# A hybrid decoder layer on eight cores: a token sweep written as a pipeline, output weights in other places, expert gathers one expert earlier

## The reference, cut to what matters

```python
h = x
hn = _rmsnorm(h, norm_mix_g[l])
proj = hn @ w_in[l]
pool_out = _pool_mixer(proj[..., :POOL_WIDTH], pool_w[l], pool_scale[l])
rwkv_out = _rwkv7_mixer(proj[..., POOL_WIDTH:], ...)
mixed = jnp.concatenate([pool_out, rwkv_out], axis=-1)
h = h + mixed @ w_out[l]
hn = _rmsnorm(h, norm_xattn_g[l])
h = h + _memory_xattn(hn, mem_n, xattn_w_q[l], xattn_w_kv[l], xattn_w_o[l])
hn = _rmsnorm(h, norm_ffn_g[l])
h = h + _hier_moe(hn, ...)      # out += gate_e * ((silu(t @ w_gate[e]) * (t @ w_up[e])) @ w_down[e])
return _rmsnorm(h, norm_final_g)
```

## Time and profile before

| | us |
|---|---|
| median of three runs | 2842.55 (2833.57 to 2846.49) |
| profiled execution | 2855.55 |
| its span on the slowest core | 2854.0 |
| spans of the eight cores | 2771.5 to 2854.0 |
| PE busy | 2296.1 (80%) |
| VectorE busy | 1410.7 (49%) |
| ScalarE busy | 1230.1 (43%) |
| software DMA queue, share of 16 DMA engines | 57.2% |
| hardware DMA queue, share of 16 DMA engines | 19.9% |

### The profile page before, as it was taken

How to read it: one execution, slowest core, us unless ns; L and a number is a source line. 1 busy time by engine, 2 the same in 40 slices (tenths; PEclk the granted TensorE clock), 3 DMA queues, 4 the chain that set the end, 5 groups by cost and what they waited for, 6 DMA issues and landing times.

```text
span 2854.0 us, 57117 instructions; the slowest of 8 cores (2771.5 to 2854.0 us)
## 1 busy us (share of the span) xinstructions
PE 2296.1 (80%) x24853; PEld 1283.7 (45%) x25144; DVE 1410.7 (49%) x2615; ACT 1230.1 (43%) x2301; POOL 348.3 (12%) x555
## 2 busy tenths in 40 slices
PE   4888889888998898997388685886885978788886
PEld 2455545554555545554134342442443544444443
DVE  3546656665666665676132321422324564555454
ACT  5546766667666765676122121221221231222322
POOL 2011111101111111110111010100000010110211
PEclk9889999999999999999599897998997989899898
DMA  9678779878786779765899898999974656666693
GB/s 175 119 124 131 135 123 138 142 122 141 127 145 119 119 132 139 122 118 162 146 140 137 145 143 144 144 140 134 150 200 173 196 170 220 193 216 201 182 196 83
DMA packets 175293, 427.32 MB, mean 150 GB/s; under 512 B 80032, under 2 KB 101024, under 8 KB 160704
## 3 DMA queue, kind: packets, MB, share of 16 engines
q0 software_dynamic: 86288, 251.00, 57.2%
q1 hardware_dynamic: 88752, 172.62, 19.9%
HBM read 598.87 MB, written 142.74 MB: 260 GB/s over the span
## 4 chain that ended last, share of the span: by engine, by line
PE 58%; DMA 14%; issue 12%; DVE 6%; ACT 5%; another core or an unknown queue 2%; POOL 2%; POOLq 0%; DVEq 0%
PE ps L128 58%; ACT big L144 5%; DVE big L151 3%; DMA big<-h_s,big 2%; DVE big L156 2%; DMA big<-x 2%; DMA big<-mixd 2%; DMA big<-w_qT 2%; DMA big<-w_kv 1%; DMA big<-w_lo 1%; DMA out<-big 1%; DMA vod<-big 1%; DMA big<-w_out 1%; POOL big L186 1%
## 5 line engine op out<-in xcount | busy, mean ns | idle before, releaser
L128 PE MATMUL ps<-big 64*64 64x64 bf16 (+8 forms) x24853 | 2296.1, 263 | 534.3 <-ACT big L144 112.3
L128 PEld LDWEIGHTS ps<-big 64*64 64x64 bf16 (+3 forms) x25144 | 1283.7, 109 | 1546.3 <-issue 243.8
L144 ACT ACTIVATE big<-big 128x512 f32<-128x512 f32 (+4 forms) x896 | 541.7, 635 | 714.9 <-DVE big L151 462.8
L151 DVE TENSOR_TENSOR big<-ps,big 128x512 bf16<-128x512 f32 (+4 forms) x656 | 466.1, 721 | 716.3 <-PE ps L128 590.6
L144 ACT ACTIVATE big<-ps 128x512 bf16<-128x512 f32 (+2 forms) x904 | 505.5, 588 | 670.9 <-PE ps L128 661.3
L144 ACT ACTIVATE big<-ps,big 128x512 f32<-128x512 f32 (+2 forms) x332 | 210.5, 649 | 216.3 <-PE ps L128 213.2
L156 DVE SCALAR_TENSOR_TENSOR big<-ps,big 128x512 f32<-128x512 f32 (+2 forms) x316 | 225.6, 722 | 111.0 <-ACT big L144 68.3
L156 DVE SCALAR_TENSOR_TENSOR big<-big 128x512 bf16<-128x512 f32 (+4 forms) x212 | 227.2, 1078 | 52.0 <-DMA big<-h_s,big 45.5
L151 DVE TENSOR_TENSOR big<-big 128x512 bf16<-128x512 f32 (+11 forms) x406 | 198.9, 511 | 93.5 <-DMA big<-w_r 50.0
L156 DVE SCALAR_TENSOR_TENSOR big<-big,ps 128x64 f32<-128x64 f32 (+1 forms) x280 | 91.9, 331 | 156.8 <-PE ps L128 154.8
L172 DVE CAST big<-ps 128x512 bf16<-128x512 f32 x168 | 109.4, 684 | 40.9 <-PE ps L128 16.3
(11 more groups left out here) (27 smaller groups left out, 215.1 us busy)
## 6 DMA issues: line engine op xcount, KB each, us to landing
big<-w_rkv POOLq DMA_DIRECT2D x96, 512.0 KB, 7.7
big<-x SPq DMA_DIRECT2D x32, 1024.0 KB, 7.8
wgc<-wg_l POOLq DMA_DIRECT2D x56, 512.0 KB, 14.9
big<-wgc SPq DMA_DIRECT2D x56, 512.0 KB, 4.3
wuc<-wu_l POOLq DMA_DIRECT2D x52, 512.0 KB, 12.6
wdc<-wd_l POOLq DMA_DIRECT2D x52, 512.0 KB, 15.4
big<-wuc SPq DMA_DIRECT2D x52, 512.0 KB, 4.8
big<-wdc SPq DMA_DIRECT2D x52, 512.0 KB, 4.8
```

The source lines that it names most:

```text
L128: r.append(e.matmul(out, lhsT=lhsT, rhs=rhs, start=st, stop=sp_, **k))
L144: return self.op("act", lambda e: e.activation(out=out, in_=in_, func=func, **kw), dur, R, W, P, tbl=TBL.get(func))
L151: return self.op(eng, lambda e: e.tensor_tensor(out=out, in0=a, in1=b, op=op), dur, R, W, P)
```

## The change

- **Planner.** One DMA rate for all queues (480), bytes counted on both sides of a transfer, and queues that overlap in time slow each other in the simulation.
- **Mixer.** `EXM` 12 becomes 20: 80 recast jobs instead of 48 stand here, 80 instead of 112 in the sweep. The 82 memory steps are spread over 27 units instead of 31.
- **Places.** The 16 pieces of w_out lie in 4 pieces of the first slot of the normalized input, 9 in the memory projections' space, 3 in the weight ring. QK lies in the second slot and in the weight ring behind w_out, VO behind it. The loads of QK and VO are written after the first two tiles' loads.
- **Sweep.** The loop body is cut into functions and written as a pipeline: norm of tile t, half the projection of t+1, scores of t, the other half, loads of t+2, routing of t-1, memory values of t. Four buffers of h instead of three; the bf16 copy goes, and the scores' transposes take the f32 rows; squares go to the mixd buffer or h2T, not to E32; `ohr` has a place of its own.
- **Experts.** Gathers stand one expert earlier, with 8 buffers instead of 6; two of the 8 PSUM banks serve the gathers alone; `wxr` has 12 pieces instead of 16, in the first 12 places of w_out.

The diff, cut to its core:

```diff
-DMA_RATE = dict(sp=220.0, act=220.0, pool=340.0)
+DMA_RATE = 480.0
...
-        nb = n * (4 if F32 in (out.dtype, in_.dtype) else 2)
+        nb = n * sum(4 if a.dtype == F32 else 2 for a in (out, in_))
...
+    def part(self, off, n):
+        b = self.alloc(off, n)
+        b.a = self.big[:, off:off + n]
+        return b
...
+                s0, w = max(c + d + DMA_LAT, dma_free[e]), o.bytes / DMA_RATE
+                e2 = max((q for q in dma_free if q != e), key=lambda q: dma_free[q])
+                ov = min(max(dma_free[e2] - s0, 0.0), 2 * w)
+                dma_free[e2] += ov / 2
+                o.end = dma_free[e] = s0 + w + ov / 2
...
-EXM, ERC = 12, 40
+EXM, ERC = 20, 40
...
-                        while done < NS and done * 31 < NS * u:
+                        while done < NS and done * 27 < NS * u:
...
+            WP = [HN_OFF + i * 1024 for i in range(4)] + [AC_OFF + i * 1024 for i in range(9)] + [WR_OFF + i * 1024 for i in range(3)]
+            wok = [S.part(o_, 1024) for o_ in WP]
+            QKh = [S.part(o_, 2048) for o_ in (HN_OFF + 4096, HN_OFF + 6144, WR_OFF + 3072, WR_OFF + 5120)]
+            VOh = [S.part(WR_OFF + 7168 + 2048 * h, 2048) for h in range(4)]
...
-            hbs = [(d_.f32(D), [Buf() for _ in range(4)]) for _ in range(3)]
-            xb, hT = d_.bf16(D), d_.bf16(D)
-            jka = E32.a.bitcast(BF16)
-            ohr = h2T
+            mxr = d_.bf16s(2, 16 * 128)
+            hbs = [(d_.f32(D), [Buf() for _ in range(4)]) for _ in range(4)]
+            hT = d_.bf16(D)
+            ohr = d_.f32(512)
...
+            def d_load(tt):
+                hb, hq = hbs[tt % 4]
+                mxb, st = mxr.next(), sst.next()
+                S.dma("sp", r3(mxb.a, 16), mixd[q_][:, :, o_:o_ + 128], R=[mixq[q_]], W=[mxb])
+                S.dma("sp", hb.a, x[tt * 128:(tt + 1) * 128, :], W=hq)
...
-                S.cp(xb.fresh().a, hb, R=hq, W=[xb])
-                S.act(jka, hb, AF.Square, R=hq, W=[E32], P=[st], accum_out=st.a[:, 0:1])
-                transposes([xb.a[:, k * 128:(k + 1) * 128] for k in range(16)], hT3, [xb], P=[hT], ring=dps)
+                S.act(mxb.a, hb, AF.Square, R=hq, W=[mxb], P=[st], accum_out=st.a[:, 0:1])
+                tposes(hb, hq, r3(hT.a, 16), hT.fresh())
...
+            d_load(0)
+            d_load(1)
+            for i in range(2):
+                S.dma("sp", QK4[0][:, i], qkd[:, i], R=[qkq[i]], W=[QKh[i]])
...
+            d_out(0, range(4))
+            for tt in range(NTT):
+                d_norm(tt)
+                if tt + 1 < NTT:
+                    d_out(tt + 1, (0, 1))
+                d_scores(tt)
+                if tt + 1 < NTT:
+                    d_out(tt + 1, (2, 3))
+                if tt + 2 < NTT:
+                    d_load(tt + 2)
+                if tt:
+                    d_route(tt - 1)
+                d_mem(tt)
+            d_route(NTT - 1)
...
-            wxr = Ring([wx.bf16(2048) for _ in range(16)])
+            wxr = Ring([S.part(o_, 1024) for o_ in WP[:12]])
-            ys = [(e_.f32(D), [Buf() for _ in range(4)]) for _ in range(6)]
+            ys = [(e_.f32(D), [Buf() for _ in range(4)]) for _ in range(8)]
-            eps_ = Ring(bank)
+            eps_, gps_ = Ring(bank[0:6]), Ring(bank[6:8])
...
-                    pb = eps_.next()
+                    pb = gps_.next()
...
-                for b in bs:
-                    if b not in bk:
-                        gather(b)
+                for b in ((3, 4) if e == 0 else (), (5,), (6, 7), (8, 9, 10))[e % 4]:
+                    if e // 4 * 6 + b < 24:
+                        gather(e // 4 * 6 + b)
...
-                if e % 4 == 2 and e < 14:
-                    for b in range(3):
-                        gather((e // 4 + 1) * 6 + b)
```

More of the change, by code:

```diff
@@ L214, in schedule @@
                     m = s.bl
-            d = o.dur if not o.bytes else DMA_LAT + o.bytes / DMA_RATE[o.eng]
+            d = o.dur if not o.bytes else DMA_LAT + o.bytes / DMA_RATE
             o.bl = m + d + LAT
@@ new lines, in build @@
+            wok = [S.part(o_, 1024) for o_ in WP]
+            wo3 = [b_.a.bitcast(BF16) for b_ in wok]
+            QKh = [S.part(o_, 2048) for o_ in (HN_OFF + 4096, HN_OFF + 6144, WR_OFF + 3072, WR_OFF + 5120)]
+            QK4 = [big[:, o_:o_ + 4096].bitcast(BF16).rearrange("p (h c m) -> p h c m", h=2, c=16) for o_ in (HN_OFF + 4096, WR_OFF + 3072)]
+            VOh = [S.part(WR_OFF + 7168 + 2048 * h, 2048) for h in range(4)]
+            VO3 = r3(big[:, WR_OFF + 7168:WR_OFF + 15360].bitcast(BF16), 8)
@@ L1095, in recast, with d_out @@
                     S.dma("pool", d_, s_, P=[bs], after=[o])
[L1097 to L1100, removed]
+            tl = {}
+            def d_load(tt):
+                hb, hq = hbs[tt % 4]
                 for b_ in hq:
                     b_.fresh()
-                mxb = mxr.next()
+                mxb, st = mxr.next(), sst.next()
                 q_, o_ = divmod(tt * 128, QT)
                 S.dma("sp", r3(mxb.a, 16), mixd[q_][:, :, o_:o_ + 128], R=[mixq[q_]], W=[mxb])
+                S.dma("sp", hb.a, x[tt * 128:(tt + 1) * 128, :], W=hq)
+                tl[tt] = (hb.a, hq, mxb, st)
+            def d_out(tt, dbs):
+                hb, hq, mxb, st = tl[tt]
                 m3 = r3(mxb.a, 16)
[L1107 to L1110, removed]
+                for db in dbs:
                     b = dps.next()
@@ L1134, in build, with d_mem @@
                     S.ts(Eb.a[:, h * 256:(h + 1) * 256], E32.a[:, h * 256:(h + 1) * 256], st.a[:, 8 + h:9 + h], ALU.mult, R=[E32, st], P=[Eb])
+            def d_mem(tt):
+                hb, hq, mxb, st = tl[tt]
                 ET3 = r3(ET.a, 8)
-                transposes([Eb.a[:, k * 128:(k + 1) * 128] for k in range(8)], ET3, [Eb], P=[ET], ring=dps)
+                transposes([Eb.a[:, k * 128:(k + 1) * 128] for k in range(8)], ET3, [Eb], P=[ET.fresh()], ring=dps)
                 for db in range(4):
@@ L1162, in build @@
                     routing(tt // 4, lgb, rsb)
+            d_load(0)
+            d_load(1)
+            for i in range(2):
+                S.dma("sp", QK4[0][:, i], qkd[:, i], R=[qkq[i]], W=[QKh[i]])
+            for i in range(2):
+                S.dma("sp", QK4[1][:, i], qkd[:, 2 + i], R=[qkq[2 + i]], W=[QKh[2 + i]])
+            for h in range(4):
+                S.dma("sp", VO3[:, 2 * h:2 * h + 2, :], vod[:, 2 * h:2 * h + 2, :], R=[voq[h]], W=[VOh[h]])
+            d_out(0, range(4))
[12 more added lines that the diff above has]
+            d_route(NTT - 1)
         def grp_cols(n):
@@ L1179, in build @@
             S.cp(flgi.a, flg.a, R=[flg], W=[flgi])
-            wx = Al(S, big, WR_OFF, WR_OFF + 16384)
-            wxr = Ring([wx.bf16(2048) for _ in range(16)])
-            e_ = Al(S, big, HN_OFF, WR_OFF)
+            wxr = Ring([S.part(o_, 1024) for o_ in WP[:12]])
+            for b_ in wxr.b:
+                b_.a = b_.a.bitcast(BF16)
+            g_ = Al(S, big, HN_OFF + 4096, AC_OFF)
+            gL, gF = g_.f32(D), g_.f32(D)
+            e_ = Al(S, big, AC_OFF + 8192, WORDS)
             XEr = Ring([e_.bf16(16 * 384) for _ in range(5)])
@@ L1191, in build @@
             jkb = xn
-            gL, gF = e_.f32(D), e_.f32(D)
             S.dma("sp", gF.a, gB[3], W=[gF])
             S.dma("sp", gL.a, gB[2], W=[gL])
-            eps_ = Ring(bank)
+            eps_, gps_ = Ring(bank[0:6]), Ring(bank[6:8])
             outd = [Buf() for _ in range(24)]
             bk, XE = {}, {}
-            yfree = list(range(6))
+            yfree = list(range(8))
             def members(e):
```

67 lines of the change are left out of this document (28 added, 39 removed).

## The result

| | before | changed |
|---|---|---|
| median of four executions, us | 2842.56 (2833.57 to 2846.49) | 2649.45 (2642.42 to 2657.1) |
| ratio | | 0.9325, 95% interval 0.9291 to 0.9360 |
| profiled execution, us | 2855.55 | 2657.1 |
| its span, slowest core | 2854.0 (core 4) | 2655.5 (core 5) |

A forecast was written before the change was run, and what follows sets the result against it. Bound in turn by PE with busy DMA, a latency chain, and the gathers' latency. Terms +10 - 30 - 60 - 57 + 0 - 58 = -195: span 2659, plus 1.55, times 0.9954 = 2648 us; range 2570 to 2770 (0.84).

The forecast's parts named there:

- Mixer: First stage: 32 more recasts, output-weight loads and earlier memory steps cost +10 us, ends +90 and -50.
- own end of +90: Mixer's slow end: 4.5 us of PE work lost per 50 us, as in the worst stretch at full DMA.
- fourth rival: Mixer cannot use more DMA than its mean share of 0.78: +252 us instead of +10, total 2890; chance 0.06.
- Hole: Between mixer and sweep: output weights arrive earlier, PE then waits for mixd; 8 of 37.8 us left, -30.
- end of -38: Hole's best case, -38 us where -30 was forecast; its other end was 0.
- Sweep's period: Token sweep: other tiles' work fills PE's idle time, a tile every 36.3 us, -60; ends -85 and -15.
- third rival: Sweep: the planner could already take the next projection early, so the period stays at 40.8 us: +60, 2708; chance 0.10.
- Sweep's stalls: Sweep: fourth buffer, earlier mixd loads and lower DMA demand leave 15 of 72.5 us, -57; ends -72 and +60.
- first rival: Sweep: mixd loads become the pace, 132 us of waits where 15 were left, total 2765; chance 0.15.
- Experts: Last stage: earlier gathers remove 73 us of group-change waits, less 10 for VectorE and 5 for weights: -58.
- second rival: Experts: gathers move the wait to VectorE, the change of group costs as before: +58, 2706; chance 0.13.

The follow-up runs named there:

- a_h3: The changed kernel with three buffers of h instead of four, the load of tile t+2 behind the routing of tile t-1; 2663.56 us.
- a_recast12: The changed kernel with 48 recasts in the mixer as before, 112 in the sweep; 2718.98 us.
- b_recast20: The kernel before with 80 recasts in the mixer instead of 48, memory-projection halves kept in order on a PSUM bank; 2872.59 us, beside 2876.38 before.
- v4direct: The changed kernel with four of each expert's 12 pieces loaded uncast: 128 recasts, 48 in the mixer, 80 in the sweep; 2599.92 us.
- a_gather_late: The changed kernel with the gathers written where they stood before, eight buffers and two PSUM banks kept; 2662.07 us.
- a_banks8: The changed kernel with all eight PSUM banks in one ring for expert work and gathers, early gathers and eight buffers kept; 2713.59 us.
- a_order: The changed kernel with one more planner constraint, keeping memory-projection matmul groups that share a PSUM bank in order, same work; 2631.02 us.

## Why the prediction was right in total and wrong in its parts

The sum of -195 was met by -190 by luck, because errors cancel. Cut where PE leaves the mixer, the mixer was put 73 us too low, hole and sweep 53 too high, the experts 22 too high, joint and tail 7 too low (73 - 53 - 22 + 7 = 5).

**Mixer: wrong, +83 for +10.** This is the mis-sized step: +83 where PE leaves the mixer, near its own end of +90, and +105 by the last chain step. The sign named for it (last matmul between 1360 and 1420; wrong beyond 1450) came out wrong at 1483 on the slowest core, 1455 on the mean of eight. It was priced by PE's work in stretches of 50 us at DMA shares of 0.98 and 0.60. Such a stretch shows what PE did with loads that had been issued well before; it does not show that each load would land later once 32 more transfers of 1 MB stand among them. The price had to be read from the landing times of the mixer's loads and from the share of its chain of waits that is DMA, 15.6% already before. A clock adds to the waits, but less than the two stage tables suggest: the 1176.82 us of core 4 lack 222 matmul records (18402, beside 18624 weight loads). On the six cores of each trace that have them all, PE's busy time in the mixer grew by 26 us, from 1204.6 to 1230.9, while the granted clock of the stage fell from 0.94 to 0.91. The other 57 us or so are waits. The fourth rival had the mechanism, DMA demand of some 1273 us that the mixer cannot absorb, and priced it at 252; the DMA share of the mixer did rise, from 0.79 to 0.89 on the mean, so the stage took most of it in, and it cost 83.

**Hole: right, at its end.** The weights were there, and what PE waited for was mixd, as forecast, but for 0.47 us where 8 were left. From 37.8 to 0.5 us is -37, for -30 with an end of -38.

**Sweep's period: right in kind, too small.** 36.3 us was forecast; 262.56 us of the chain of waits carry eight tiles, 32.8 each, below the 35 to 38 named as a sign. Both allowances were too large: PE has no idle of 1.5 us per tile left (525.7 of 531 busy), and its work per tile shrank, where 0.6 us more were allowed: those 32.8 us hold what took 34.2. Over 14 periods, routing included, it fell from 35.5 to 33.3 us (means of eight cores), with a granted clock of 0.95 before and 1.00 now while PE works. The third rival, that the planner had found all this already, is out.

**Sweep's stalls: right in size, wrong in reason.** 4.9 us of mixd waits are left where 15 were allowed. The forecast credited the fourth buffer; a_h3 shows that it does next to nothing. The fall in DMA demand, named second, is the cause, and a_recast12 shows the first rival in full when the recasts stay: mixd 146.3 us late in total, with a sweep of 678 us. The Trainium skill ("DMA: Bandwidth & Descriptors", Queues, rings and completion order) has a DMA engine change between queues only at packet boundaries; the runs agree in direction and show no single packet: the loads of mixd land in 28.1 us in the median in a_recast12 and in 20.6 in the changed kernel, at software-queue shares of 68.6% and 61.6%. Over the loads of all eight cores it is 43.6 and 20.8 us, and in the old loop 21.4 before and 11.1 in b_recast20, so in both pairs fewer recasts go with earlier landings.

**What the sum could not show: the two edits need each other.** Period, stalls and recasts were costed as terms that add. Alone they give -72 and -44, together -222. The recasts' move costs 62 (old kernel) to 85 us (changed) in the mixer and is worth 150 in the pipelined sweep (678 - 528), but only 44 in the old one.

**Experts: right in kind, -80 for -58.** The waits at the changes of group went as forecast. The sign named for it, no wait over 3 us at a change, held but for waits of 3.91 and 12.80 us. The 10 us set aside for VectorE's fixed order did not appear, nor did the 5 for the shorter weight ring: PE's waits of the stage (14.6, 12.3, 2.4 and 1.0 us) end on VectorE and ScalarE, none on weights. One late gather of 12.80 us stands in their place. The reason, gathers written an expert earlier, was wrong: buffers and banks hold them, the text does not. The second rival is out.

**Tail: not foreseen, +6.** From POOL's last scatter (issued by 2634.7) there are 20.8 us to the end, where there were 13.9. Tails come in steps over these kernels: 22 to 23 us with 48 recasts in the mixer (before, a_recast12, v4direct), 29 to 30 with 64 or 80, 36 in a_gather_late and a_banks8. No run tells why; it stays open.

## What to carry to other kernels

A transfer moved beside latency-bound work is priced by what it does to the landing of the loads already there and by how much of that stage's chain is DMA, not by whether the busiest engine keeps busy next to a full DMA system. Where two edits act on one stage, work out the load of each resource with both and with each alone: the one that goes over decides, and gains then do not add. Under a scheduler that reorders freely, an operation's place in the text need not be a constraint (the gathers' was none); look for the buffer or bank that is. And where stages overlap, the place of the cut between them moves time from one to the other: 20 us here.

## What the runs showed of the hardware beyond expectation

- The granted clock was 0.99 over 531 us of sweep and 0.98 over 557 us of experts with PE nearly never idle, on the slowest core with all eight cores at the same work, against 0.91 and 0.93 with waits between. These figures count the idle stretches. While PE works, it was 0.95 in the sweep before, 0.98 in a_recast12 and 1.00 in the changed kernel (means of eight cores over 14 periods). From a_recast12 to the changed kernel, which do the same work on PE, a period fell by 10.4 us (44.6 to 34.2): 9.5 of idle and 0.9 of PE's work (34.2 to 33.3). A wait taken from PE gave back a little more than its own length.
- In the mixer, loads on the hardware queue land later when the software queue has more to do: x, 1 MB, took 7.0 us in the median at a software share of 67.6%, 12.5 at 82.6%, 7.3 at 71.2%. It is no rule for every stage: in the sweep x took 8.3 us at 68.6% (a_recast12) and 12.2 at 61.6% (changed).
- A changed order of equal work moved the mixer by about 20 us on the mean of eight cores (a_order). Differences of that size between two planned kernels say nothing of their edits.
